# Dense matmuls of a streaming encoder trunk: 640 token columns split as 512 and 128 in place of 320 and 320

## The reference

```python
for l in range(DEPTH):                       # DEPTH = 2
    h = _rmsnorm(x, norm_mix[l])
    if l % 2 == 0:                           # HGRN2 heads and retention heads
        z = h @ w_in0                        # 1024 -> 4096
        ...
        x = x + mix @ w_out0                 # 1024 -> 1024
    else:                                    # xLSTM mLSTM block
        up = h @ w_up1                       # 1024 -> 4096
        ...
        x = x + (hC * silu(zg)) @ w_down1    # 2048 -> 1024
    h = _rmsnorm(x, norm_ffn[l])
    x = x + (silu(h @ w_ffn_gate[l]) * (h @ w_ffn_up[l])) @ w_ffn_down[l]   # 1024 -> 2816 -> 1024
y = _rmsnorm(x, norm_final)
```

## Time and profile before

| | us |
|---|---|
| three runs | 2413.48, 2416.87, 2416.16; median 2416.16 |
| profiled execution, span from first to last instruction | 2413.6 |
| TensorE busy | 2257.1 (94% of the span) |
| weight loads busy | 1992.1 (83%) |
| DVE, POOL, ACT busy | 1006.7, 843.3, 474.3 |
| DMA | mean 93 GB/s |

### The profile page before, as it was taken

How to read it: one execution, slowest core, us unless ns; L and a number is a source line. 1 busy time by engine, 2 the same in 40 slices (tenths; PEclk the granted TensorE clock), 3 DMA queues, 4 the chain that set the end, 5 groups by cost and what they waited for, 6 DMA issues and landing times.

```text
span 2413.6 us, 35270 instructions
## 1 busy us (share of the span) xinstructions
PE 2257.1 (94%) x13637; PEld 1992.1 (83%) x13637; DVE 1006.7 (42%) x1339; ACT 474.3 (20%) x695; POOL 843.3 (35%) x492
## 2 busy tenths in 40 slices
PE   6999997899999998999999899898979899999997
PEld 5898996899999998999576464645549899999996
DVE  5564565522220126891226557475652322220025
ACT  4343333211100012111221312313110111110011
POOL 4333231445445455554111001010115454454543
PEclk9999998999999999999999999898989999999998
DMA  4121221122222222323122506052351112222222
GB/s 163 59 80 54 93 76 45 61 70 70 78 76 72 79 70 103 109 78 110 47 105 105 213 28 260 29 208 110 117 206 70 70 62 77 77 71 79 70 78 87
DMA packets 57296, 224.24 MB, mean 93 GB/s; under 512 B 6289, under 2 KB 11281, under 8 KB 48273
## 3 DMA queue, kind: packets, MB, share of 16 engines
q1 hardware_dynamic: 48576, 202.94, 23.5%
q10 hardware_dynamic: 8656, 20.39, 2.3%
HBM read 170.06 MB, written 53.25 MB: 93 GB/s over the span
## 4 chain that ended last, share of the span: by engine, by line
PE 78%; DVE 10%; DMA 4%; issue 4%; ACT 3%; DVEq 1%; POOL 0%; SPq 0%; ACTq 0%; POOLq 0%
PE psd L203 9%; PE psd L207 9%; PE psd L208 9%; PE psd L204 9%; PE psd L210 9%; PE psd L209 9%; DMA Cs<-st_c 3%; PE psm L1208 3%; DVE cv L900 2%; PE psm L1179 2%; PE psd L1117 2%; DVE ntmp L276 2%; PE psm L381 2%; PE psm L1080 1%; PE psm L1215 1%
## 5 line engine op out<-in xcount | busy, mean ns | idle before, releaser
L1713 POOL CAST whi<-wraw 128x1024 fp32r<-128x1024 f32 x224 | 236.5, 1056 | 995.5 <-PE psd L210 531.2
L1715 POOL TENSOR_TENSOR wlo<-wraw,whi 128x1024 fp32r<-128x1024 f32 x224 | 543.9, 2428 | 17.9
L203 PE MATMUL psd<-xh,whi 128*128 128x320 f32 x1280 | 407.1, 318 | 31.8 <-ACT xh L249 19.1
L207 PE MATMUL psd<-xl,whi 128*128 128x320 f32 x1280 | 402.3, 314 | 12.1 <-POOL xl L284 9.9
L204 PE MATMUL psd<-xh,whi 128*128 128x320 f32 x1280 | 399.1, 312 | 0.0
L208 PE MATMUL psd<-xl,whi 128*128 128x320 f32 x1280 | 398.7, 311 | 0.0
L209 PE MATMUL psd<-xh,wlo 128*128 128x320 f32 x1280 | 398.6, 311 | 0.0
L210 PE MATMUL psd<-xh,wlo 128*128 128x320 f32 x1280 | 398.5, 311 | 0.0
L203 PEld LDWEIGHTS psd<-xh,whi 128*128 128x128 f32 x1280 | 243.7, 190 | 35.9 <-issue 29.4
L207 PEld LDWEIGHTS psd<-xl,whi 128*128 128x128 f32 x1280 | 243.2, 190 | 20.0 <-POOL xl L284 14.6
L204 PEld LDWEIGHTS psd<-xh,whi 128*128 128x128 f32 x1280 | 244.1, 191 | 0.7
(11 more groups left out here) (352 smaller groups left out, 3412.9 us busy)
## 6 DMA issues: line engine op xcount, KB each, us to landing
wraw<-w SPq DMA_DIRECT2D x224, 512.0 KB, 3.2
Cs<-st_c SPq DMA_DIRECT2D x32, 1024.0 KB, 6.7
c_s<-Cs SPq DMA_DIRECT2D x32, 1024.0 KB, 4.6
z_kept<-zb ACTq DMA_DIRECT2D x16, 320.0 KB, 2.2
ztp<-z_kept SPq DMA_DIRECT2D x4, 1024.0 KB, 5.5
c_p<-Cp SPq DMA_DIRECT2D x4, 1024.0 KB, 3.9
xT<-x SPq DMA_DIRECT2D x4, 640.0 KB, 6.7
x_kept<-xT ACTq DMA_DIRECT2D x1, 2560.0 KB, 8.6
```

Of the source, the lines that this page charges most:

```text
L203: pe.matmul(o0, wh, x0, start=st, stop=False)
L207: pe.matmul(o0, wh, l0, start=False, stop=False)
L1713: pool.tensor_copy(whi[s][:], wraw[s][:]).then_inc(w_high, 1)
L1715: pool.tensor_tensor(wlo[s][:], wraw[s][:], whi[s][:].bitcast(F32), ALU.subtract).then_inc(w_split, 1)
```

## The change

The pair is cut at 512 in place of 320: the first matmul of each pair takes the 512 prompt columns, the second the 128 columns of the streams. The results then lie side by side in PSUM (`pD` is `psd` seen as one row of 1024 columns), and every evacuation reads 640 columns in one stretch. `evac_x` needs one copy for the prompt part in place of two. The norms' matmuls are cut in the same way. The head norms (L427, L428) and rotations (L449 to L453) keep 320 and 320.

```diff
             # halves
-            return t[:, k, 0:HT], t[:, k, HT:T]
+            return t[:, k, 0:SEQ], t[:, k, SEQ:T]
...
             # pe_dense
-                o0, o1 = psd[pair][:, 0, 0:HT], psd[pair][:, 1, 0:HT]
+                o0, o1 = pD[pair][:, 0:SEQ], pD[pair][:, SEQ:T]
...
             # Norm.act
-                a.activation(two(rstd[:]), psd[self.g % 2][:, :, 0:HT], ACT.Ln, bias=eps,
+                a.activation(rstd[:], pD[self.g % 2][:, 0:T], ACT.Ln, bias=eps,
...
             # Norm.pe
-                p.matmul(o[:, 0, 0:HT], ones, nacc[:, 0:HT], start=True, stop=False)
-                p.matmul(o[:, 1, 0:HT], ones, nacc[:, HT:T], start=True, stop=False)
+                p.matmul(o[:, 0:SEQ], ones, nacc[:, 0:SEQ], start=True, stop=False)
+                p.matmul(o[:, SEQ:T], ones, nacc[:, SEQ:T], start=True, stop=False)
...
             # in0_evac; gate_tile and the FFN's silu likewise
-            a.activation(two(dst[:]), psd[g % 2][:, :, 0:HT], func, scale=scale).then_inc(z_done.sem, 1)
+            a.activation(dst[:], pD[g % 2][:, 0:T], func, scale=scale).then_inc(z_done.sem, 1)
...
             # evac_x
-                src = psd[g % 2]
-                a.activation(dst[:, NCONV - 1:NCONV - 1 + HT], src[:, 0, 0:HT], ACT.Copy)
-                a.activation(dst[:, NCONV - 1 + HT:NCONV - 1 + SEQ], src[:, 1, 0:SEQ - HT], ACT.Copy)
-                a.activation(streams(dst, NCONV - 1, TS), src[:, 1, SEQ - HT:HT].rearrange("p (b c) -> p b c", c=TS),
+                src = pD[g % 2]
+                a.activation(dst[:, NCONV - 1:NCONV - 1 + SEQ], src[:, 0:SEQ], ACT.Copy)
+                a.activation(streams(dst, NCONV - 1, TS), src[:, SEQ:T].rearrange("p (b c) -> p b c", c=TS),
...
             # vec_residual; the FFN's product likewise
-                v.tensor_tensor(x, x, psd[(g0 + s) % 2][:, :, 0:HT], ALU.add).then_inc(evac[(g0 + s) % 2], 1)
+                v.tensor_tensor(x, x, pD[(g0 + s) % 2][:, 0:T], ALU.add).then_inc(evac[(g0 + s) % 2], 1)
```

More of the change, by code:

```diff
@@ L161, in trunk @@
         psm = ctx.enter_context(nc.psum_tensor("psm", [P, 4, 512], F32))
+        flat = lambda p: p.rearrange("p a c -> p (a c)")
+        pD = [flat(psd[s][:, :, :]) for s in range(2)]
         w_loaded = [sem(f"w_loaded{s}") for s in range(2)]
@@ L299, in pe @@
             def pe(self, p):
-                o = psd[self.g % 2]
+                o = pD[self.g % 2]
                 p.wait_ge(self.acc_done, KD)
@@ L303, in pe @@
                     p.wait_ge(evac[self.g % 2], self.g // 2)
-                p.matmul(o[:, 0, 0:HT], ones, nacc[:, 0:HT], start=True, stop=False)
-                p.matmul(o[:, 1, 0:HT], ones, nacc[:, HT:T], start=True, stop=False)
+                p.matmul(o[:, 0:SEQ], ones, nacc[:, 0:SEQ], start=True, stop=False)
+                p.matmul(o[:, SEQ:T], ones, nacc[:, SEQ:T], start=True, stop=False)
                 p.wait_ge(self.sq_done, KD)
                 last = sq[(KD - 1) % 2]
-                p.matmul(o[:, 0, 0:HT], ones, last[:, 0:HT], start=False, stop=True)
-                p.matmul(o[:, 1, 0:HT], ones, last[:, HT:T], start=False, stop=True).then_inc(self.sum_done, 1)
+                p.matmul(o[:, 0:SEQ], ones, last[:, 0:SEQ], start=False, stop=True)
+                p.matmul(o[:, SEQ:T], ones, last[:, SEQ:T], start=False, stop=True).then_inc(self.sum_done, 1)
         G_N0 = 0
@@ L787, in trunk @@
         assert r3[0] <= 229312, r3[0]
-        flat = lambda p: p.rearrange("p a c -> p (a c)")
-        pD = [flat(psd[s][:, :, :]) for s in range(2)]
         pM = [flat(psm[:, 2 * s:2 * s + 2, :]) for s in range(2)]
@@ L932, in gate_tile @@
                         a.wait_ge(self.zst[s], 16 * i)
-                    a.activation(two(zb[s][:]), psd[g % 2][:, :, 0:HT], ACT.Silu).then_inc(evac[g % 2], 1)
+                    a.activation(zb[s][:], pD[g % 2][:, 0:T], ACT.Silu).then_inc(evac[g % 2], 1)
                     a.wait_ge(evac[g % 2], g // 2 + i + 1)
@@ L1591, in tile @@
                 v.wait_ge(pe_unit, units[0] + units[1] * (2 * i + s + 1))
-                x = xT[:, bass.ds(2 * i + s, 1), :].rearrange("p a (c d) -> p (a c) d", c=2)
-                v.tensor_tensor(x, x, psd[(g0 + s) % 2][:, :, 0:HT], ALU.add).then_inc(evac[(g0 + s) % 2], 1)
+                x = xT[:, bass.ds(2 * i + s, 1), :].rearrange("p a c -> p (a c)")
+                v.tensor_tensor(x, x, pD[(g0 + s) % 2][:, 0:T], ALU.add).then_inc(evac[(g0 + s) % 2], 1)
                 if norm is not None:
@@ L1637, in act @@
                             a.wait_ge(pe_unit, u + 4 * i + 2 * s + 1)
-                            a.activation(two(ffs[s][:]), psd[gg % 2][:, :, 0:HT], ACT.Silu).then_inc(evac[gg % 2], 1)
+                            a.activation(ffs[s][:], pD[gg % 2][:, 0:T], ACT.Silu).then_inc(evac[gg % 2], 1)
                             a.wait_ge(evac[(gg + 1) % 2], (gg + 1) // 2 + 2 * i + 1)
@@ L1651, in vec @@
                             v.wait_ge(pe_unit, u + 4 * i + 2 * s + 2)
-                            v.tensor_tensor(two(fft[s][:]), two(ffs[s][:]), psd[(gg + 1) % 2][:, :, 0:HT],
+                            v.tensor_tensor(fft[s][:], ffs[s][:], pD[(gg + 1) % 2][:, 0:T],
                                             ALU.mult).then_inc(evac[(gg + 1) % 2], 1)
```

## The result

| | before | changed |
|---|---|---|
| median of the runs | 2414.82 us (4 runs) | 2641.52 us (4 runs, 2637.09 to 2645.12) |
| ratio | | 1.094, 95% interval 1.0924 to 1.0958 |
| span of the profiled execution | 2413.6 us | 2635.3 us |

A forecast was written before the change was run, and what follows sets the result against it. TensorE was taken to bound the kernel, by a matmul's stream or the next one's weight load. 2413.6 + 260.8 - 9 = 2665.4 us, with 2.6 us for the median 2668 us; range 2595 to 2840.

The forecast's parts named there:

- step 4: Waits behind four norms (4.7 us) and among layer 0's heads (about 4 us) hide part of the loss: together -9 us.
- The bound: Dense FFN stretches: TensorE sets the pace, bounded by the running matmul's stream or the next weights' load, whichever ends later.
- Step 2: Narrow matmul of each pair: lasts as long as the next wide one's weight load, 115.7 ns (111.3 to 120, beyond it 146.3).
- Step 1: Wide matmul of each pair: 213.3 ns of stream plus a fixed 13 ns, 226.3 ns (ends 216.0 and 233.9).
- Step 3: Each dense pair: 342.0 ns against 292.6 before, 49.4 ns more, for 5280 pairs +260.8 us.
- Steps 5 and 6: Norms' 20 float32 matmuls: 0.1 us in all, nothing; evacuations: 640 elements read as before, nothing saved on the path.
- Step 7: Granted clock: TensorE never idles and narrow float32 matmuls run at a granted clock of 1.00, so nothing added.
- No floor: Rival, dense pairs: a matmul costs its stream plus a constant at any width, so time stays at 2416 us; chance 0.05.
- Loads that run ahead: Rival, narrow matmul: the next wide load begins before the narrow stream, so -108 us, 2308 us; chance 0.03.
- Narrow fp32r in two passes: Rival: a 128-column fp32r matmul takes two passes with a load each, 228.4 ns, some 3263 us; chance 0.08.

The follow-up runs named there:

- the cuts: Changed kernel with pairs cut at 448 and 192, then 384 and 256 columns: 2507.01 us (1.0394 of before) and 2415.60 us (1.0011).
- the half loads: Only 64 weight columns loaded and used in each k-step's second and third pairs, cut at 512 or 320: 2493.73 us and 2404.80 us.
- short512: Changed kernel (512 and 128) with only 64 weight columns in each k-step's second and third pairs (third not in a unit's last): 2493.73 us, 1.0338 of before.
- cut384: Changed kernel with the pair cut at 384 and 256 columns in place of 512 and 128: 2415.60 us, 1.0011 of before.
- lay320: Changed kernel's layout and copies, but pairs cut at 320 and 320 as before: 2412.88 us, 1.000 of before.

## Why the prediction was right, point by point

2668 us were forecast, 2641.5 measured, with the sign, the mechanism and the place as said. Three terms of the sum were mis-sized, and two of them cancelled, which was luck. The loss was forecast 25 us too high: with 47.4 ns a pair, the FFN's measured price, in place of 49.4, some 11 us of that are the pair's price and the other 14 are step 4.

- **The bound.** TensorE sets the pace in the dense stretches, and a slot is the longer of its own stream and the next one's load: shown by the cuts and by the half loads.
- **Step 2, the narrow matmul (115.7 ns taken).** Too much. From the start of the load beside a narrow matmul to that of the next, the mean in the steady FFN (580 to 900 us) is 108.6 ns, under the low end of 111.3 from float32 rows; the 120 of the earlier trace rows was no guide.
- **Step 1, the wide matmul (226.3 ns taken, 13 over the stream).** Too little, and this is the step that failed: "the excess has no reason to grow once the load is over". It grows with the columns. In short512 (600 to 900 us), where the load beside it is of 64 columns, a wide matmul of 512 takes 231.6 ns, 18 over its stream, and a narrow one of 128 takes 59.7, 6 over. In cut384 the means of the same stretch are 175.9 ns for 384 and 117.5 for 256 columns, before 146.3 for 320. All are 0.452 to 0.466 ns a column, and half the load takes 1 ns off the 320 ones, no more. So it was not the load's doing, and the truth lay near the upper end of step 1, 233.9.
- **Step 3, the pair.** 342.0 forecast; 108.6 + 232.7, the mean from the load that begins with the wide stream to the next, is 341.3. The two errors, 7 ns too much and 6 ns too little, cancel.
- **Step 4, what is hidden (9 us taken).** Too little. At the FFN's 47.4 ns, 5280 pairs are 250 us, and 222 arrived between the traces: 28 us were hidden (24 by the medians). Layer 0's mixers hid 14 of them (forecast: 4 and a part of 4.7); TensorE's waits there, from 30 us to the last head, add up to 19.9 us before and 12.1 after. The up projection hid 11, for which the forecast had "nothing else hides it"; the earlier trace rows already named "ACT zb L933 5.5", and 2.5 us for the lower clock came behind it. The mLSTM heads came out 4.8 us shorter with no dense matmul in them, which one execution of each cannot give to the change: over the profiled executions of all kernels here this stage takes 557 to 565 us, the short ones with 60 us of it at the 1.2 GHz level and the longest with 76.
- **Steps 5 and 6.** Norms and evacuations: nothing, as said. lay320 came at 1.000, and from the last norm's first matmul to the end it is 19.9 us in both profiled executions. The norms' own cut was run in no kernel by itself.
- **Step 7, the clock (nothing taken).** Right for the dense stretches, at 1.00 in the FFN. Over the whole kernel it was not nothing: the mean granted clock was 0.969 before and 0.977 after, by the same estimate 150 us at the 1.2 GHz level before and 121 after. The 29 us are worth up to 14 us, which is part of what step 4 calls hidden. How much of that the change does, by shorter waits, and how much is the chance of one execution is not shown; the kernel before had 0.967 to 0.973 in its runs.
- **The rivals.** No floor: out, short512 shows it. Loads that run ahead: out, none of the 10560 loads of the dense matmuls begins before the matmul directly ahead of its own. Narrow fp32r in two passes: out, 1280 records per line as before, and 59 ns of stream for 128 columns. The Trainium skill's pace of 81 ns at 128 and 131 ns at 512 columns ("TensorE: Matmul & The Clock Gate", "Back-to-back issue gap") is off for fp32r at both ends, where 108.6 and 232.7 ns were measured. The Trainium skill's formula for a weight load, on the same page in the section "LDWEIGHTS (loading the stationary operand)", columns over 1.2, gives 106.7 ns for 128 columns; 108.6 was measured.

## What to carry to other kernels

Where every matmul brings its own weights, a matmul's slot (the time from its start to the next one's) is the longer of its stream and the next one's load: cut the free dimension so that no piece streams for less than the load, and even halves are safe where wide-and-rest is not. Here 256 fp32r columns were enough for 128 columns of weights and 192 were not; full-width pieces gain next to nothing, since streaming costs nearly the same per column at any width. And ask of each hidden cost what covers it: slower dense units gave back 28 of 250 us, much of it in places where TensorE had been waiting for others, which also showed where the kernel before could be made 7 us faster. An idle stretch can cost more than its length: 5.5 us of waiting cost 8, by the lower clock behind it.

## What the runs showed of the hardware that was not expected

At the full granted clock an fp32r matmul of 320 columns takes 0.457 ns a column, 1.10 cycles of 2.4 GHz, and a record of plain float32 takes 429 ns for what I read as 1024 cycles, 1.006 each. The start of the kernel before, at the 1.2 GHz level (granted clock 0.50 from 22 to 27 us), shows the same fp32r matmul without this excess (timeline):

```profile
23.90 0.47 PE L209 MATMUL psd<-xh,wlo 128*128 128x320 f32 x1
...
24.16 0.47 PE L210 MATMUL psd<-xh,wlo 128*128 128x320 f32 x1
...
24.43 0.47 PE L203 MATMUL psd<-xh,whi 128*128 128x320 f32 x1
...
24.70 0.47 PE L204 MATMUL psd<-xh,whi 128*128 128x320 f32 x1
```

There it is 0.267 us for 320 columns, 320 / 1.2 to the nanosecond. The excess is no contention with the other engines either: in the kernel before, matmuls of the first FFN during which VectorE, ScalarE and GpSimd all rest come at 146.3 ns, and the 48 beside all three at 146.6. What makes it stays open.

An uneven pair is dearer still at the 1.2 GHz level. At the start of the changed kernel's down projection (granted clock 0.50 from 1925 to 1930 us) the timeline shows:

```profile
1927.56 0.74 PE L210 MATMUL psd<-al,whi 128*128 128x512 f32 x1
1928.09 0.31 PE L211 MATMUL psd<-al,whi 128*128 128x128 f32 x1
1928.20 0.74 PE L212 MATMUL psd<-ah,wlo 128*128 128x512 f32 x1
...
1931.40 0.73 PE L210 MATMUL psd<-al,whi 128*128 128x512 f32 x1
```

Six pairs take 3.84 us, 640 ns each, where two even matmuls take 533: 107 ns more, against 48 at full clock. With 512 / 1.2 = 427 ns for the wide stream, an estimate of 213 is left for the narrow matmul and the load beside it, where 108.6 was measured at full clock: the load too is slower at the lower clock.
